# First SSM group of a hybrid decoder: the time step's sums moved from VectorE to GpSimd

## The reference

```python
proj = u @ w_in                                   # 1024 -> z 2048, xBC 3072, dt 32
xbc_act = silu(conv4(xbc) + conv_b)               # depthwise, 4 taps
dtf = softplus(dt + dt_bias)                      # (tokens, 32 heads)
A = -exp(a_log)
a_cum = cumsum(dtf * A, within a chunk of 128)
# y_diag, y_off, chunk states: use exp of differences of a_cum, and x * dtf
y = rmsnorm_per_group((y + d_skip * x) * silu(z)) * norm_w
out = y @ w_out
```

## Time and profile before

| | us |
|---|---|
| median of 3 runs | 968.6 (967.44 to 968.86) |
| the profiled execution, own time | 967.62 |
| its span, first to last instruction | 965.8 |
| PE busy | 945.0 (98%) |
| DVE busy | 547.2 (57%) |
| ACT busy | 478.4 (50%) |
| POOL busy | 318.5 (33%) |

### The profile page before, as it was taken

How to read it: one execution, slowest core, us unless ns; L and a number is a source line. 1 busy time by engine, 2 the same in 40 slices (tenths; PEclk the granted TensorE clock), 3 DMA queues, 4 the chain that set the end, 5 groups by cost and what they waited for, 6 DMA issues and landing times.

```text
span 965.8 us, 18482 instructions
## 1 busy us (share of the span) xinstructions
PE 945.0 (98%) x7288; PEld 877.0 (91%) x7288; DVE 547.2 (57%) x1416; ACT 478.4 (50%) x943; POOL 318.5 (33%) x257
## 2 busy tenths in 40 slices
PE   9999999999999999999999999999999999999998
PEld 8998899989998999979988889998899988998787
DVE  4234421534234421456688678856698566985783
ACT  6335713464235613377346665256562565626852
POOL 3442234233342244226533224422344223442500
PEclk9999999999999999999999999999999999999999
DMA  7522222322224221212424714357232563416403
GB/s 210 180 73 91 63 88 75 125 112 88 82 79 150 89 88 56 83 23 59 142 91 129 226 49 141 89 148 205 67 124 90 156 197 87 137 56 209 113 12 104
DMA packets 144614, 105.91 MB, mean 110 GB/s; under 512 B 10754, under 2 KB 135860, under 8 KB 144464
## 3 DMA queue, kind: packets, MB, share of 16 engines
q1 hardware_dynamic: 134536, 100.19, 34.2%
q10 hardware_dynamic: 9992, 4.54, 2.0%
HBM read 91.99 MB, written 16.79 MB: 113 GB/s over the span
## 4 chain that ended last, share of the span: by engine, by line
PE 85%; DVE 9%; issue 2%; ACT 2%; DMA 1%; POOL 1%; SPq 0%; DVEq 0%; ACTq 0%; POOLq 0%
PE pp L1279 21%; PE pp L1281 20%; PE pp L1280 20%; PE pS L1389 2%; PE pO L1613 2%; PE pO L1609 2%; PE pT_ L1599 2%; PE pS L1620 2%; PE pO L1436 1%; PE pO L1435 1%; DVE s_in L2288 1%; PE pO L1560 1%; PE pS L1532 1%; DVE cv L2011 1%; PE pS L1570 1%
## 5 line engine op out<-in xcount | busy, mean ns | idle before, releaser
L705 POOL TENSOR_TENSOR w_lo_buf<-w_raw_buf,w_hi_buf 128x512 fp32r<-128x512 f32 x214 | 274.8, 1315 | 470.0 <-ACT w_hi_buf L781 290.3
L1279 PE MATMUL pp<-h_hi,w_hi_buf 128*128 128x280 f32 (+2 forms) x1248 | 377.0, 302 | 1.9 <-DVE rb L1985 1.6
L1281 PE MATMUL pp<-h_hi,w_lo_buf 128*128 128x280 f32 (+2 forms) x1248 | 362.7, 291 | 0.0
L1280 PE MATMUL pp<-h_lo,w_hi_buf 128*128 128x280 f32 (+2 forms) x1248 | 362.1, 290 | 0.0
L1279 PEld LDWEIGHTS pp<-h_hi,w_hi_buf 128*128 128x128 f32 x1248 | 234.8, 188 | 10.9 <-issue 7.7
L1280 PEld LDWEIGHTS pp<-h_lo,w_hi_buf 128*128 128x128 f32 x1248 | 234.9, 188 | 4.6 <-issue 4.1
L1281 PEld LDWEIGHTS pp<-h_hi,w_lo_buf 128*128 128x128 f32 x1248 | 235.1, 188 | 0.0
L781 ACT ACTIVATE w_hi_buf<-w_raw_buf 128x2048 fp32r<-128x2048 f32 (+1 forms) x55 | 104.1, 1892 | 34.7 <-DMA w_raw_buf<-in_w_ssm_in 23.7
L1791 DVE TENSOR_TENSOR x<-x,pp 128x272 f32<-128x272 f32 (+2 forms) x120 | 53.1, 442 | 81.6 <-PE pp L1281 81.0
L1279 PE MATMUL pp<-og_hi,w_hi_buf 128*128 128x280 f32 (+2 forms) x256 | 75.5, 295 | 2.8 <-DVE x L1791 1.1
L1281 PE MATMUL pp<-og_hi,w_lo_buf 128*128 128x280 f32 (+2 forms) x256 | 74.4, 291 | 0.0
(11 more groups left out here) (353 smaller groups left out, 1614.9 us busy)
## 6 DMA issues: line engine op xcount, KB each, us to landing
w_raw_buf<-in_w_attn_in SPq DMA_DIRECT2D x16, 1024.0 KB, 5.2
w_raw_buf<-in_w_ssm_in SPq DMA_DIRECT2D x16, 1024.0 KB, 5.7
w_raw_buf<-in_w_attn_out SPq DMA_DIRECT2D x8, 1024.0 KB, 5.3
s_in<-in_state_ssm SPq DMA_DIRECT2D x32, 256.0 KB, 4.5
out<-s_in SPq DMA_DIRECT2D x32, 256.0 KB, 3.0
w_raw_buf<-in_w_ssm_out SPq DMA_DIRECT2D x8, 1024.0 KB, 6.7
seg<-a_scratch SPq DMA_DIRECT2D x12, 512.0 KB, 5.1
w_raw_buf<-in_w_attn_in SPq DMA_DIRECT2D x8, 512.0 KB, 6.4
```

The source lines that it names most:

```text
L705: ins = pool.tensor_tensor(low_buf(n)[:, piece], raw[n % RAW_SLOTS][:, piece], high_buf(n)[:, piece].bitcast(F32), ALU.subtract)
L1279: pe.matmul(dst, hi[:, k, cols], a_hi[:, k, tk], start=(k == 0), stop=False)
L1280: pe.matmul(dst, hi[:, k, cols], a_lo[:, k, tk], start=False, stop=False)
L1281: mm = pe.matmul(dst, lo[:, k, cols], a_hi[:, k, tk], start=False, stop=(k == depth - 1))
```

## The change

On POOL, `split_lo` of slab bc is called by itself. Then POOL waits for DVE's product (`dt_mid`, counted by L1963) and for ACT (`dt_ln`), adds `t4`, adds `t1` (relu), and multiplies by A, which is broadcast along the tokens; each of the three counts `dt_sum` and the next waits for it. Only then does it go on to `split_lo` of x0, x1 and z0. `dt_third` on DVE keeps only the scan, behind a wait for `dt_sum` of 3, and is called ahead of `conv_taps(g, 2)`, where it stood behind `conv_in(g, 3, 0)`. `conv_in(g, 4, 0)` is called ahead of the building of `ea_in` and `dec_in`, where it was the first step of `conv(g, 4)` behind them. POOL's wait ahead of z1 is for `xw_done` of 1 (the end of `prepare(0, 0)`'s main part) in place of `conv_done` of 6.

```diff
+            split_lo(slab_no[("bc", GROUPS, 0)] + 1)
+            pool.wait_ge(dt_mid, 1)
+            pool.wait_ge(dt_ln, 1)
+            pool.tensor_tensor(dtT[:, :], dtT[:, :], t4[:, :], ALU.add).then_inc(dt_sum, 1)
+            pool.wait_ge(dt_sum, 1)
+            pool.tensor_tensor(dtT[:, :], dtT[:, :], t1[:, :], ALU.add).then_inc(dt_sum, 1)
+            pool.wait_ge(neg_a, 1)
+            pool.wait_ge(dt_sum, 2)
+            pool.tensor_tensor(t1[:, :], dtT[:, :], aneg[:, :].to_broadcast([32, T]), ALU.mult).then_inc(dt_sum, 1)
             for g in range(GROUPS):
                 s = GROUPS + g
                 split_lo(slab_no[("z", s, 1)] + (1 if g else 0))
                 for u in range(UNITS):
                     if g == 0 and u == 1:
-                        pool.wait_ge(conv_done, 6)
+                        pool.wait_ge(xw_done, 1)
                         split_lo(slab_no[("z", s, 1)] + 1)
...
                 dve.wait_ge(dt_ln, 1)
-                link(dve.tensor_tensor(dtT[:, :], dtT[:, :], aT[:, :], ALU.mult))
+                dve.tensor_tensor(dtT[:, :], dtT[:, :], aT[:, :], ALU.mult).then_inc(dt_mid, 1)
 
             def dt_third():
-                link(dve.tensor_tensor(dtT[:, :], dtT[:, :], t4[:, :], ALU.add))
-                link(dve.tensor_tensor(dtT[:, :], dtT[:, :], t1[:, :], ALU.add))
-
-                dve.wait_ge(neg_a, 1)
-                link(dve.tensor_scalar(t1[:, :], dtT[:, :], aneg[:, :], None, ALU.mult))
+                dve.wait_ge(dt_sum, 3)
                 dve.tensor_tensor_scan(aT[:, :], cst[0:32, C_RESET:C_RESET + T], t1[:, :], 0.0,
                                        ALU.mult, ALU.add).then_inc(a_ready, 1)
...
                     conv_in(g, 2, 1)
+                    dt_third()
                     conv_taps(g, 2)
                     conv_in(g, 3, 0)
...
                 if g == 0:
-                    dt_third()
                     conv_in(g, 3, 1)
                     conv_taps(g, 3)
+                    conv_in(g, 4, 0)
...
-                    conv(g, 4)
+                    conv_in(g, 4, 1)
+                    conv_taps(g, 4)
```

## The result

| | before | after |
|---|---|---|
| median, us (lowest to highest), runs | 968.02 (967.31 to 968.86), 4 | 978.97 (978.39 to 979.86), 4 |
| ratio after to before, 95% interval | | 1.0114 (1.0101 to 1.0126) |
| profiled execution, own time and span | 967.62 and 965.8 | 979.86 and 978.0 |
| mean granted clock | | 0.992 |

The change makes the kernel 11 us slower. The prediction said slower, 972.5 with a range of 968.8 to 976.5. Its direction held, its size did not. Three executions in these experiments (one each of before, sums_128 and z1_wait) ran at a mean granted clock of 0.85 or less and took 1028 to 1537 us; medians and ratios leave them out.

The account below looks back on a forecast made before the run. PE sets the pace up to 487, DVE from there to 515. Stall +4.9, clock +1.9, vanished PE waits -1.9, `prepare` -1.0 make +3.9 on 968.6: 972.5 us, range 968.8 to 976.5.

Parts of the forecast that it names:

- The order and x0's time: POOL in group 0: x0's split stands behind sums of 4.5 us, so its low part is ready at 485.7.
- its late bound: Latest time for x0's low part on POOL, with the split at its slowest: 487.1.
- The stall: PE ahead of x tile 0 waits for x0's low part from 480.78 to 485.7: 4.9 us (4.4 to 6.3).
- The collision rival: POOL and DVE slow each other beside the taps of tiles 0 and 1, 0.8 us an instruction: 975.5, chance 0.19.
- The clock: PE's clock falls inside the stall, and slow matmuls after it lose 1.9 us (lower bound 0).
- The rival in which it holds: Same stall at x tile 0, but PE's clock stays up and no matmuls are slow: 970.6, chance 0.26.
- What DVE's relief gives back: DVE drops the sums, so PE's waits of 1.64 at 502.28 and 0.25 at 493.33 vanish: 1.9 us saved.
- `prepare`: In `prepare(0, 0)`, L2083 no longer runs beside z1's split on POOL: 1.0 us saved (0 to 1.0).

Follow-up runs that it names:

- sums_128: The change with its three POOL sums on 128 partitions in place of 32, no pause added; median 972.94 us, ratio 1.0053.
- z1_wait: The kernel before with only POOL's wait ahead of z1's split moved to `xw_done`; median 966.89 us, ratio 0.9989.
- pause: The change plus one POOL wait for its own third sum ahead of x0's split; median 973.14 us, ratio 1.0057.
- late_x0: The kernel before with x0's split on POOL waiting for DVE's product, no sums on POOL; median 971.52 us, ratio 1.0041.
- x0_first: The change with x0's split moved ahead of the three POOL sums; median 969.08 us, ratio 1.0004.
- pool_run: The kernel before plus eight unread 128x512 subtractions back to back on POOL from DVE's product on; median 972.15 us, ratio 1.0034.
- filled: The change plus 88 unread matmuls on PE ahead of x tile 0; median 977.83 us, ratio 1.0095.
- gaps: The change plus six POOL waits between the pieces of the splits of x0 and x1; median 973.90 us, ratio 1.0057.
- sums_early: z1_wait plus sums and scan on DVE between the halves of x tile 0, and x tile 2's bank evacuated early; median 969.55 us, ratio 1.0020.
- run_32: pool_run with the third of its eight subtractions on 32 partitions; one run, 974.65 us.
- run_32_broadcast: pool_run with its third subtraction made a product on 32 partitions with a broadcast operand; one run, 975.67 us.
- run_32_last: pool_run with the last of its eight subtractions, directly ahead of x1's split, on 32 partitions; one run, 975.64 us.
- run_broadcast: pool_run with the third of its eight subtractions taking a broadcast operand, on 128 partitions; one run, 971.30 us.

## Why the prediction was right or wrong

**The order and x0's time: right, in part by luck.** The sums run from 476.74 to 481.47, 4.7 us against 4.5. x0's four pieces are half of the 9.80 us from 481.47, which puts its low part at 486.4; less 0.77 that is 485.6, against 485.7 in the prediction. But it was reached because DVE stood still and POOL ran at its own pace. With DVE running (pause) it is 487.15 - 476.09 + 476.0 = 487.1 on the prediction's clock, its late bound.

**The stall: the step that failed.** I made the stall from x0 alone and said "nothing hides it". A half of PE waits for two things, the slab and the bank, and I followed only the first. The bank comes from DVE: its evacuation ends at 483.6 in pause but at 493.1 in after, 6.7 us behind x0. The term was 4.9 (at most 6.3), and it measured 11.56. The shut-out is 11.56 - 6.11 = 5.4 us of that by PE's waits and 978.97 - 973.14 = 5.8 by the medians.

**The collision rival: right in mechanism, wrong in place and price.** It said that DVE's instructions beside POOL's run would be held up by 0.8 us each and "still end before PE hands over x tile 0 half 1". The normal price is 0.7 to 1.0 us each, so that was sized well. But the taps of tile 0 are due before x tile 0 half 0, not half 1, since that half wants the bank that L1991 empties. late_x0 and x0_first show that even the normal price makes PE wait there, 2.79 and 1.82 us. And nothing in the trace of before had a DVE instruction held for more than one of POOL's (longest 1.92 us), so a wait through nine was outside every bound that I had. The Trainium skill's page "SBUF — State Buffer" (Who interferes with whom) is firmer than the page that I had used: the pair of ports that DVE and GpSimd share is an exclusive lock, "the other **fully blocks**" for a whole instruction. The alternation in pool_run agrees with it (1.5 us a tap, not 0.83). On who gets the lock it says "Issue order, not op shape, decides who blocks", and this case's rows do not agree: the tap that began at 480.57 stood behind eight subtractions that began from 481.47 on, was passed over at eight ends of POOL instructions and let in only at the ninth, and whether that happens goes with the number of partitions of POOL's instruction.

**The clock: right.** It fell 3.1 us after PE fell idle, as the earlier trace rows had it, and cost 2.4 us by the spacing of the matmuls, 2.1 by filled, against 1.9. (4.3 x 3/7 is 1.84, so the term should have read 1.8; and the earlier trace rows holds 40 matmuls, not 20. Neither moves the forecast by more than 0.1.) The rival in which it holds, the first of the three, fell. The 3 us are no fixed delay: in gaps the clock fell 2.0 us after PE fell idle (480.42), in x0_first it fell about 1 us after PE had taken up work again (483.09). What I had not seen is that much shorter waits bring it down too (below).

**What DVE's relief gives back: right.** PE's waits of 1.64 and 0.25 us are gone. A new loss of 0.6 us at the conv transposes was not in the sum (1.39 against 0.76). x0_first has 1.39 as well, and so has sums_early, where POOL does no sum. late_x0 keeps before's order on DVE and has 0.8. So it goes with the new order of scan and banks; which of these edits does it was not tried.

**`prepare`: right**, 1.0 us by L1580 (0.24 against 1.27) and by z1_wait.

**The sum with the measured terms.** For pause, which is the change without the shut-out: 6.1 (stall) + 1.6 (slow matmuls until about 490.8) - 1.9 - 1.0 + 0.6 = +5.4, and its ratio of 1.0057 is +5.5. For the change: 11.6 + 2.4 - 1.9 - 1.0 + 0.6 = +11.7, and 1.0114 is +11.0 (9.8 to 12.2). So without the shut-out the forecast of 972.5 would have missed by 0.6 us and lain inside its range.

**What stays open.** A narrow POOL instruction in an unbroken run is what the five kernels with a full shut-out (after, filled, run_32, run_32_broadcast, run_32_last) and gaps as far as its first pause have in common, and the six without it lack one or the other: pool_run, run_broadcast and late_x0 have no narrow one, sums_128 has widened it, pause breaks the run, and in x0_first the run ends with the sums. Why it has this effect is not settled. Nor is why in run_32 it set in only at the step to the split, five instructions later, while in after it set in at the same step with the narrow ones directly ahead.

## What to carry to other kernels

When GpSimd work is moved, list what DVE runs beside it in its new place and count 0.7 to 1.0 us more for each long DVE instruction from SBUF (here 0.52 or 0.83 us alone), and 0.3 to 0.5 more for each GpSimd instruction (here 1.25 alone); then check every buffer that PE waits for, banks as well as weights. Where a GpSimd instruction on 32 partitions is followed at once by more GpSimd work, and DVE works beside it, try a wait between them or 128 partitions: either was worth some 5.5 us here. And a short wait of PE can cost nearly twice itself when the clock falls with it (1.8 + 1.5 us in x0_first).

## What the hardware did that I had not expected

- One DVE tap of 0.83 us took 11.34, held through POOL's third sum and eight subtractions, after a POOL instruction on 32 partitions; the same with 128 partitions, 1.57 (sums_128). A single wait on POOL cures it (pause, 1.57).
- Fewer partitions make POOL no faster: the first sum took 1.38 us with 32x560 and 1.39 with 128x560 in sums_128, the least of the earlier trace rows for 128x560.
- DVE's instructions with an operand in PSUM show no such stretching beside POOL: the evacuation at 483.18 in pause took 0.44 us beside x0's split, and the 16 instances of L2296 (L2288 of before) at 534.7 to 540.8 in after took 339 to 347 ns, those beside z1's split among them.'s 329 to 349 ns alone would not have shown it, since in before only 2 of the 128 instances touch a POOL instruction.
- The granted clock fell after waits of PE of no more than 1.82 us (x0_first), 2.48 (pool_run), 2.72 (sums_early) and 2.79 (late_x0), while in before it held through 1.64. In x0_first it cost 1.5 us on top of the 1.8.
- The length of the wait doesn't decide by itself. The same transposes follow a wait of 1.69 us in after and in late_x0:

```profile
929.97 1.09 PE L1609 MATMUL pT_<-seg,xdt 128*64 128x128 f32 x16 [1.69 <-issue]
...
921.07 1.61 PE L1602 MATMUL pT_<-seg,xdt 128*64 128x128 f32 x16 [1.69 <-issue]
```

  In after (the first row) the clock stayed at 1.00; in late_x0 it fell at about 921.5 and stood at 0.50 from 922 to 924. What decides between the two is open.
